# Cached attention of a decoder layer in half quads between the w_in tiles, and prompt heads in a pipeline of their own

## The reference, cut to what matters

```
x = x + 0.5*gt1 * swiglu(modulate(x, g_ffn1, sh1, sc1))      # w1, w3: 2048 x 5504, w2: 5504 x 2048
z = modulate(x, g_mix, sh2, sc2) @ w_in                      # w_in: 2048 x 6152
qa, ka, va, fa, qb, kb, vb = split(z); q and k through rmsnorm per head
fox heads (8):     softmax(q k / sqrt(128) + cum(log_sigmoid(fa + b))) v    # prompt: causal; sample: 1024 cached keys
dilated heads (8): three windows (128 by 1, 512 by 4, 2048 by 16) combined  # sample: cached window of 1024 keys
x = x + gt2 * (heads @ w_out)                                # w_out: 2048 x 2048
x = x + 0.5*gt3 * swiglu(modulate(x, g_ffn2, sh3, sc3))
```

## Time and profile before

| | |
|---|---|
| three runs | 2617.25, 2620.0, 2620.32 us; median 2620.0 us |
| the profiled execution | 2615.63 us, its span 2613.6 us |
| TensorE busy, weight loads busy | 2462.6 us (94%), 2337.3 us (89%) |
| VectorE, ScalarE busy | 1163.9 us (45%), 905.1 us (35%) |
[...]
| moved by DMA | 614.5 MB, mean 235 GB/s |

### The profile page before, as it was taken

One profiled execution on the slowest core, in us unless ns is written; L12 is line 12 of the kernel. 1 busy time (PEld: TensorE's weight loads), 2 busy tenths in 40 slices (PEclk: granted clock), 3 DMA queues, 4 the chain that ended last, 5 costly groups with the idle time before them and its releaser, 6 DMA issues.

```text
span 2613.6 us, 56953 instructions
## 1 busy us (share of the span) xinstructions
PE 2462.6 (94%) x23011; PEld 2337.3 (89%) x23011; DVE 1163.9 (45%) x1802; ACT 905.1 (35%) x1099; POOL 45.2 (2%) x87
## 2 busy tenths in 40 slices
PE   5899999999999998999998766897999999999999
PEld 4899999999999998999995434697999999999999
DVE  2343444444443456666641112455444444454444
ACT  2333222332223334666521112335333333333332
POOL 0031000000000000000000000000000000000000
PEclk8999999999999999999998979998999999999999
DMA  8988777777877754444558999743444544454444
GB/s 333 397 308 310 272 296 287 290 275 291 301 284 295 273 177 145 143 147 160 197 197 311 393 377 407 287 171 117 160 163 165 171 160 165 160 172 161 167 159 160
DMA packets 111330, 614.51 MB, mean 235 GB/s; under 512 B 16248, under 2 KB 22672, under 8 KB 62336
## 3 DMA queue, kind: packets, MB, share of 16 engines
q1 hardware_dynamic: 107136, 603.81, 63.0%
q0 software_dynamic: 4096, 9.27, 1.0%
HBM read 605.93 MB, written 8.67 MB: 235 GB/s over the span
## 4 chain that ended last, share of the span: by engine, by line
PE 87%; DMA 7%; SPq 2%; DVE 1%; ACT 1%; issue 1%; ACTq 0%; DVEq 0%
PE banks L621 26%; PE banks L622 26%; PE banks L623 25%; PE banks L541 5%; DMA adax<-in_w_ada_dram 2%; SPq L474 1%; DMA kv_h<-in_vpool_dram 1%; PE banks L892 1%; DMA kv_raw<-in_wink_dram 1%; DMA kv_z<-in_wink_dram 1%; PE banks L849 1%; SPq L465 1%; PE banks L711 1%; DMA adaw<-in_w_ada_dram 1%; PE banks L589 0%
## 5 line engine op out<-in xcount | busy, mean ns | idle before, releaser
L621 PE MATMUL banks<-h_hi,w_hi 128*128 128x288 f32 x3696 | 1095.1, 296 | 26.5 <-DVE h_lo L1207 21.4
L622 PE MATMUL banks<-h_lo,w_hi 128*128 128x288 f32 x3696 | 1092.7, 296 | 0.0
L623 PE MATMUL banks<-h_hi,w_lo 128*128 128x288 f32 x3696 | 1091.7, 295 | 0.0
L1175 DVE TENSOR_TENSOR w_lo<-raw,w_hi 128x1024 fp32r<-128x1024 f32 (+2 forms) x670 | 764.1, 1181 | 482.4 <-ACT w_hi L930 475.0
L930 ACT ACTIVATE w_hi<-raw 128x1024 fp32r<-128x1024 f32 (+2 forms) x670 | 673.5, 1026 | 804.0 <-PE banks L623 599.4
L621 PEld LDWEIGHTS banks<-h_hi,w_hi 128*128 128x128 f32 x3696 | 697.3, 189 | 37.0 <-issue 33.1
L622 PEld LDWEIGHTS banks<-h_lo,w_hi 128*128 128x128 f32 x3696 | 697.1, 189 | 0.8
L623 PEld LDWEIGHTS banks<-h_hi,w_lo 128*128 128x128 f32 x3696 | 696.8, 189 | 0.0
L621 PE MATMUL banks<-g_hi,w_hi 128*128 128x288 f32 x1376 | 408.6, 297 | 0.0
L622 PE MATMUL banks<-g_lo,w_hi 128*128 128x288 f32 x1376 | 406.8, 296 | 0.0
L623 PE MATMUL banks<-g_hi,w_lo 128*128 128x288 f32 x1376 | 406.6, 295 | 0.0
(11 more groups left out here) (201 smaller groups left out, 1138.0 us busy)
## 6 DMA issues: line engine op xcount, KB each, us to landing
raw<-in_w_dram SPq DMA_DIRECT2D x166, 1024.0 KB, 4.9
adaw<-in_w_ada_dram SPq DMA_DIRECT2D x112, 1024.0 KB, 6.8
raw<-in_w_dram SPq DMA_DIRECT2D x64, 896.0 KB, 4.5
raw<-in_w_in_dram SPq DMA_DIRECT2D x49, 1024.0 KB, 4.9
adax<-in_w_ada_dram SPq DMA_DIRECT2D x32, 1024.0 KB, 12.8
raw<-in_w_dram SPq DMA_DIRECT2D x32, 960.0 KB, 4.8
raw<-in_w_out_dram SPq DMA_DIRECT2D x16, 1024.0 KB, 4.9
kv_raw<-in_kpool_dram SPq DMA_DIRECT2D x24, 512.0 KB, 6.9
```

Source lines behind the costliest of these rows:

```text
L621: pe.matmul(bank[:, 0:T], hi, m_hi[:, k, :], start=k == 0, stop=False)
L622: pe.matmul(bank[:, 0:T], hi, m_lo[:, k, :], start=False, stop=False)
L623: last = pe.matmul(bank[:, 0:T], lo, m_hi[:, k, :], start=False, stop=k == nk - 1)
L1175: dve.tensor_tensor(w_lo[:, r, a:b], raw[:, r, a:b], w_hi[:, r, a:b].bitcast(F32), ALU.subtract).then_inc(S["lo_ready"], 1)
```

## The change

- The samples' attention is cut in half quads (1 MB: one page of 4 sequences, 4 heads or 512 value columns; four DMAs of 256 KB, 2 KB per partition), 104 of them. `WHERE` gives each a place: after the first or second half of a w_in tile (points 0 to 3 of a pair), or in one of three places of a step of the prompt heads. 74 lie in pairs 6 to 23, 30 in the steps.
- Pairs of w_in come in another order (`PAIR_Z`), with the gate tile ahead of pair 4, and every pair is written out rather than looped.
- Biases, new keys, turns, new values and outputs of the four groups have places of their own (`BIAS_AT`, `NEW_AT`, `TURN_AT`, `LAST_AT`, `OUT_AT`).
- `x` is stored to DRAM at the third tile and loaded back at the end; its space, parts of `z` not yet written, and `lfr`, `lfc` are buffers of half quads (`HOME`: A to E). After the last w_in tile, `w_hi` and `w_lo` are four more (W to Z).
- SP issues after slot t the half quads whose buffer was last used by the end of tile t-2; each waits for `kv_used`, and slot t+1 is behind it.
- The 16 prompt heads come after the last w_in tile, one per step, `p_turn` one step and `p_outputs` two steps behind `p_scores`.
- The first two w_out tiles wait in `raw` ahead of the last steps.

```diff
+PAIR_Z = (0, 2, 4, 6, 8, 10, 12, 14, 32, 34, 36, 38, 16, 18, 20, 22, 24, 26, 28, 30, 40, 42, 44, 46)
+NORMED = (0, 1, 2, 3, 4, 5, 6, 7, 12, 13, 14, 15, 16, 17, 18, 19)
...
+def quad_halves():
...
+    def bodies(a, b):
+        return [(at_point(i, k), 1 + (k == 1)) for i in range(a, b) for k in range(4)]
+
+    put(*[(at_point(b, k), 1) for b in range(6, 10) for k in range(4)])
+    put((at_point(11, 1), 2), (at_point(11, 2), 1), (at_point(11, 3), 1), *bodies(12, 14), (at_point(14, 0), 2))
+    put((at_point(14, 1), 1), (at_point(14, 2), 1), (at_point(14, 3), 1), *bodies(15, 17),
+        (at_point(17, 0), 2), (at_point(17, 1), 1))
+    put((at_point(18, 1), 2), (at_point(18, 2), 1), (at_point(18, 3), 1), *bodies(19, 21), (at_point(21, 0), 2))
+    put((at_point(21, 1), 1), (at_point(21, 2), 1), (at_point(21, 3), 1), *bodies(22, 23), (at_point(23, 0), 2))
+    put(*[(at_step(s, k), 1) for s in range(0, 5) for k in range(2)])
+    put(*[(at_step(s, k), 1) for s in range(5, 10) for k in range(2)])
+    put((at_step(12, 2), 1), *[(at_step(s, k), 1) for s in range(13, 16) for k in range(3)])
...
+BIAS_AT = (at_point(6, 0), at_point(14, 1), at_point(21, 1), at_step(5, 0))
+NEW_AT = (at_point(10, 1), at_point(17, 1), at_point(23, 1), at_step(10, 0))
+TURN_AT = (at_point(10, 3), at_point(17, 3), at_point(23, 3), at_step(12, 0))
+LAST_AT = (at_point(14, 0), at_point(21, 0), at_step(4, 2), at_step(15, 2))
+OUT_AT = (at_point(14, 3), at_point(21, 3), at_step(6, 2), at_step(17, 1))
+VN_AT = (at_point(12, 1), at_step(0, 0))
...
+            free = "ABCD" if spot < at_point(16, 0) else "ABCE" if spot < at_point(20, 0) else "ABE"
+            name = min(free, key=lambda n: last.get(n, -1))
...
+            name = "AB"[m - first] if m - first < 2 else "WXYZA"[(m - first - 2) % 5]
...
+            def load_half(m):
...
+                if before(m) is not None:
+                    sp.wait_ge(S["kv_used"], before(m) + 1)
...
+                for j in range(GB):
                     if kind == 0:
-                        src = (vpool if v else kpool)[bass.ds(pg[j], 1), :, :]
+                        i = (GB * g + j) * PAGES + p
+                        pg = sp.value_load(pages[0:1, i:i + 1], min_val=0, max_val=POOL - 1)
+                        src = (vpool if v else kpool)[bass.ds(pg, 1), :, 512 * c:512 * c + 512]
...
+            for t in range(TILES):
+                slot(mix, t, 0)
+                if t == 2:
+                    sp.wait_ge(S["acc_b_read"], mix.rb)
+                    sp.dma_start(x_dram, x[:, :, :]).then_inc(S["x_stored"], 16)
...
+                b = (t - 3) // 2
+                spot = at_point(b, 2 * (t - 3 - 2 * b) + 1)
+                while m < HALVES and (before(m) is None or WHERE[before(m)] <= spot) and HOME[m] not in "WXYZ" \
+                        and (HOME[m] != "E" or BIAS_AT[1] < spot):
+                    load_half(m)
+                    m += 1
+            for m in range(m, FIRST_OF[3] + 2 * WT):
+                load_half(m)
+            slot(out, 0, 0)
+            slot(out, 1, 0)
+            for m in range(FIRST_OF[3] + 2 * WT, HALVES):
+                load_half(m)
+            sp.wait_ge(S["kv_used"], last_in("A") + 1)
+            sp.dma_start(x[:, 0:7, :], x_dram[:, 0:7, :]).then_inc(S["x_back"], 16)
...
+            pool.wait_ge(S["kv_used"], last_in("B") + 1)
             pool.dma_start(toe[:, :, :], ...
...
+                    for q in range(2):
+                        pe.wait_ge(S["lo_ready"], 2 * n + q + 1)
+                        products((acc_a, acc_b)[j], n % 2, h_hi, h_lo, q * KT // 2, (q + 1) * KT // 2, KT)\
+                            .then_inc(S["w_used"], 1)
+                        if j == 1 and q == 0 and b - 1 in NORMED:
+                            head_sums(b - 1)
+                        sides(at_point(b, 2 * j + q))
...
+            for s in range(2 * HEADS + 2):
+                if s < 2 * HEADS:
+                    p_scores(s)
+                    p_values(s)
+                sides(at_step(s, 0))
+                if 1 <= s <= 2 * HEADS:
+                    p_turn(s - 1)
+                sides(at_step(s, 1))
+                if s >= 2:
+                    p_outputs(s - 2)
+                sides(at_step(s, 2))
```

More of the change, by code:

```diff
@@ L118, in plan @@
         sqs += s.bodies if s.squares else 0
-        slot += STEPS0 if s.kind == "first" else 2 * s.bodies + (s.kind == "fa")
+        slot += STEPS0 if s.kind == "first" else 2 * s.bodies + (s.kind == "mix")
         body += s.bodies
@@ new lines, with homes @@
+LF_AT, NCUM_AT = at_point(6, 2), at_point(22, 0)
+def homes():
+    names, last = [], {}
+    for m, spot in enumerate(WHERE):
+        if spot < END:
+            free = "ABCD" if spot < at_point(16, 0) else "ABCE" if spot < at_point(20, 0) else "ABE"
+            name = min(free, key=lambda n: last.get(n, -1))
+        else:
+            first = WHERE.index(at_step(0, 0))
+            name = "AB"[m - first] if m - first < 2 else "WXYZA"[(m - first - 2) % 5]
+        names.append(name)
+        last[name] = m
+    return names
@@ L129, with before, last_in @@
+HOME = homes()
+def before(m):
+    return max((i for i in range(m) if HOME[i] == HOME[m]), default=None)
+def last_in(*names, until=HALVES):
+    return max(i for i in range(until) if HOME[i] in names)
 class Chain:
@@ L234, in decoder_layer @@
[L234 to L259, removed]
@@ new lines, in decoder_layer, with home @@
+        assert over + 4224 + 4608 + 2304 <= hf0 + 2 * 2 * SQL * T * 4
+        toe = at("toe", [P, HEADS, 2 * P], F32, x0 + 8192)
+        vnat = at("vnat", [P, 2, 2 * P], F32, x0 + 16384)
+        selw = at("selw", [HEADS, HEADS * P], F32, big0 + 4 * C_BAND)
+        bias_w = at("bias_w", [P, P], F32, c0 + 1280)
+        lfn_w = at("lfn_w", [TS, P], F32, ba0)
+        def home(name, *offs):
+            n = GB // len(offs)
+            parts = [at(f"kv_{name}{i}", [P, n, 4 * P], F32, o) for i, o in enumerate(offs)]
+            return [parts[j // n][:, j % n, :] for j in range(GB)]
@@ L305, in decoder_layer @@
         KIND = (dict(n=PAGES, q=0, k=8, v=32, new=C_NEW_FOX), dict(n=WT, q=16, k=24, v=40, new=C_NEW_DIL))
[L306 to L310, removed]
+        SIDES = 2 * GROUPS
+        FIRST_OF = (0, 4 * PAGES, 8 * PAGES, 8 * PAGES + 4 * WT)
         GROUPS_ADA = ADA // GROUP
@@ L479, in _ @@
+            stream([out], 1)
             stream(segs[segs.index(out) + 1:])
@@ new lines, in side_out, with turn_v_new @@
+            def side_out(G):
+                pe.wait_ge(S["os_ready"], G + 1)
+                for h in range(HEADS):
+                    last = turn(bank[6 + h // 4][:, (h % 4) * P:(h % 4 + 1) * P], ps[:, h * P:(h + 1) * P])
+                last.then_inc(S["ot_ready"], 1)
+            def turn_v_new(kind):
+                pe.wait_ge(S["acc_b_read"], done(23 if kind else 11))
+                pe.wait_ge(S["ss_read"], 2 + HEADS * (kind + 1))
+                for c in range(2):
+                    for h in range(4):
+                        last = turn(bank[4 + c][0:TS, h * P:(h + 1) * P], z[:, KIND[kind]["v"] + 4 * c + h, TP:T])
+                    last.then_inc(S["vn_sum"], 1)
@@ L908, in _ @@
-            for kind in (0, 1):
-                for g in range(GROUPS):
-                    group(kind, g)
+            for s in range(2 * HEADS + 2):
[9 more added lines that the diff above has]
+                sides(at_step(s, 2))
@@ L1077, in p_exp @@
+            sides([at_point(PAIRS - 1, k) for k in range(4)])
             def p_exp(t):
@@ L1156, in _ @@
+            act.wait_ge(S["kv_used"], last_in("Y", "Z") + 1)
             split_high(out, 1, 0)
```

827 lines of the change are left out of this document (427 added, 400 removed).

## The result

The changed kernel takes 2595.7 us (median of four runs, 2593.1 to 2600.2) beside 2620.2 for the kernel before in the same session: ratio 0.9909 with an interval of 0.9896 to 0.9923. It is faster by 0.9%, clear of the noise, and inside the range, but the gain is 24.5 us where 64 were forecast.

The account below looks back on a forecast made before the run. TensorE bounds the w_in stage, the transfer of cached keys and values the attention stage. Overlapping them frees 101.6 us less 37 of stalls, gaining 64.6: 2615.6 becomes 2551, plus 4.4 for the median, predicted 2556 us; range 2530 to 2600.

Parts of the forecast that it names:

- the second rival: Page-number loads or landings dearer, tiles wait for weights, clock falls; stalls 60 to 95 us, 2578 to 2613; chance 0.22.
- 505.4 of work: Second w_in pair to first w_out pair: TensorE's work in us, summed from profile rows, unchanged by the change.
- 2 for the clock: Stretch from second w_in to first w_out pair: 2 us among the 37 us of new stalls.
- the dilated stretch: (21,1) to (23,0): no page numbers, three buffers, transfers needing 419 GB/s over 408; 3 us of stall.
- the SP term: Three fox stretches, pairs 11 to 21: SP's issuing of half quads slower than TensorE; stalls of 8.4, 4 and 7.7 us.
- it does not come on top: Weight slots behind half quads in SP's queue: chain of 17 us per two tiles within the 22.4 period, nothing added.
- four half quads are ahead when a stretch begins: Start of a stretch: buffers four deep, so of sixteen half quads only twelve are behind the first use.
- the halves only split the DMAs and their waits: TensorE's work in the stretch: cutting quads into halves neither adds nor removes any; 0 us.
- The third rival: Half quads' 256 KB transfers with 2 KB rows lose rate; slower below 295 GB/s, 2716 us at 250; chance 0.05.
- Bound (b): 2 KB rows, shown by no row: 408 GB/s taken; at 370 the dilated stretch and steps lose some 8 us.
- The first rival: Full overlap, only the steps' ends show: stalls 10 to 17 us, gain 85 to 91, 2529 to 2535; chance 0.12.
- The signs that the prediction named: Right: stretch about 542 us, pairs 12 to 20 at 21 to 22.5, SP never idling; wrong: TensorE waiting for `w_lo`.

Follow-up runs that it names:

- without page numbers: Changed kernel with no page number loaded: sequence b, page p reads pool page 8 b + p, same bytes and rows; 2548.7 us, ratio 0.9724.
- ScalarE's weights: Changed kernel with weight tiles from the tenth on issued from ScalarE's queue, behind the split of the tile before; 2575.8 us, ratio 0.9825.
- The two attempts to take joints away: w_in half quads only behind whole tiles: 2572.1 us atop one load per page and first four half quads spread; 2562.2 us atop no page numbers.

## Why the prediction was right in its direction and wrong in its size

The direction and the range came true, the range by the part of it that was put there for the second rival, not by the forecast's own sum. The forecast of the stretch was 505.4 of work, about 35 of idling and 2 for the clock. Measured are 541.2 of work and 47.6 of idling. By place, the steps took 103.3 us for 97, and as long without page numbers (103.0), so the queue has no part in that; the pairs took 485.5 us for 445. (The last step from the sum to the forecast is rounded up: 2551 + 4.4 is 2555.4.) By kind, the 46.8 us between 542 and 588.8 divide so:

1. **Idling, +13.** The steps and handovers (10.0 us of idling) and the dilated stretch (1.4 for 3) were forecast well or too high. The step that failed is the SP term, 20.1 us for the fox stretches with nothing added for the weight slots; 35.6 came. Its parts were right: a fox half quad takes SP 4.45 us for 4.28 forecast, its DMAs keep up, and SP ran without a pause from 1159 to 1238 us. The sum of the half quads alone was right too, as ScalarE's weights show (17.5). Wrong was the sentence on the weights, "it does not come on top". It compared periods, 17 us for two tiles with 22.4 for the queue, both as means over a pair. The queue isn't even: one to three half quads, and once four, stand ahead of a weight slot (14.3 us and 17.5 us in the two places shown), and the weights' chain behind it (landing 6.6 to 8.0, with 5 to 6 taken; the splits 2.3) has a tile's time and no more. The prediction named the four empty buffers ("four half quads are ahead when a stretch begins") as a help and did not ask what stands behind them in the queue; that alone is the wait of 5.6 us in pair 4, and 5.0 us more follow in pair 10, for which it had no term. It also left out who else waits behind a late weight: ScalarE's copies, which the program has behind the split, 8.24 us in one place. Putting the weights on another queue alone gives back 20 us.
2. **Half speed, +17.** The sum has 2 us for the clock, a term that no run shows. What the runs showed in its place: the same matmuls cost 19.0 us more in the changed kernel, at a granted clock of 0.95 in the stretch, than without page numbers, at 0.99. The wait of 8.24 us is followed by two half quads at 1.9 us instead of 1.0 and by products 0.24 apart instead of 0.13; since single late arrivals set the end, and not SP's mean period, nothing hides this time.
3. **Switching, +17.** The work without page numbers is 522.2 us for 505.4 from the rows of before, with the clock at 0.99. The rows of before came from long runs. Cut up, a run of 24 products takes 3.37 us for 3.18, one of 48 takes 6.55 for 6.36, and a half quad 1.00 to 1.05 for 0.96. Counted from start to start in that run, products take 312.0 us for 298.2, of which 12.7 lie at the ends of the 72 runs, and half quads 105.0 for 99.8, two of them at half speed; the small parts take 2.2 less than forecast. That is the 16.8. The prediction set this at 0 ("the halves only split the DMAs and their waits"). Pairs 7 and 8 show it with no wait in them: 18.5 us each, where the prediction gave 17.5. The two attempts to take joints away don't show its price in their totals (in one the work fell by 3.9 us for 15 joints, where 15 x 0.19 is 2.9, in the other it did not fall), but they do in the ends of their runs, as said there.

Of the rivals, the second, weights late, is what happened: TensorE waits for `w_lo`, the clock falls (0.50 behind the two waits shown), and 2595.7 lies in its 2578 to 2613. Its conditions were named as a dearer page-number load or a landing; the load was hardly dearer (4.45 for 4.28), the landing was (7.6 us median for a weight tile), but it is not the cause, since tiles that land in 8.8 us arrive in time once SP has no page numbers to load. The order of the queue and its length ahead of a weight slot did it. The third rival, transfers that lose their rate, fell: 293 GB/s from 1156 to 1500 us in the changed kernel is SP's doing, for the same transfers move at 337 once SP is free, and at 391 to 409 in 13 of the 40 slices of that stretch, about two thirds of whose bytes are in pieces of 256 KB. One DMA of 1 MB in place of four changed nothing for the dilated half quads (2548.4 us for 2549.1). Bound (b), 370 GB/s for rows of 2 KB, was too cautious, by the same slices of 391 to 409. The first rival, full overlap at 2529 to 2535, would have been the case with SP unburdened and no price for switching: the floor is 2548.

The signs that the prediction named held where they concerned the mechanism (SP's issues without idling in the fox stretches) and gave it away where they concerned the waits: `w_lo` and what is behind it has more of the waiting in the fox stretches (22.4 us) than the half quads (12.9). The pairs' period was forecast at 21 to 22.5 us throughout. Two tiles in a row take 19.3 us where nothing is late (so TensorE's own part is that, not 18.5), and across the wait of 8.24 us 27.2, where the run without page numbers takes 16.7 for the same two.

## What to carry to other kernels

When loads of different urgency share one queue, compare not their mean periods (22.4 us for 17 here) but the longest group that can stand ahead of the urgent one (17.5 us of half quads ahead of a weight tile), and follow who waits behind it, also on an engine whose program has other work behind the late part (ScalarE's copies, 8.24 us). An instruction that only fetches an index, 0.55 us here, is part of the transfer's cost when it is issued from the same queue: fetch it once and keep it (30 us for 128 loads less). Price TensorE's work from rows with runs as long as those the change will leave (24 products took 3.37 us, not 3.18).

## What the runs showed that was not expected

Adding 35 us of page-number loads to SP's queue (64 of 0.55 us) costs 34.7 us, one for one by the medians. Taking away the first 70 us of them gives back 30, the other 70 us 17 more: the price of a load falls as the queue gets room. Half speed is a second price of the waits, 19.0 us beside 31.2 of idling between the two kernels, and it is not in proportion to a wait: 8.24 us of idling were followed by 5.1 us at a granted clock of 0.50, 1.98 us by 9.4 us at 0.50. And a short run of products has a fixed cost: about 0.19 us for each of them, whether it is 24, 48 or 96 long (12.90 for 12.69). The kernel before pays it 18 times in this stretch, the changed kernel 72 times.
